# Norm rates on two columns: sums, reciprocal and root with tokens as rows, spread by a product with the identity

## The reference

```python
def _rmsnorm(x, w):
    xf = x.astype(jnp.float32)
    y = xf * lax.rsqrt(jnp.mean(xf * xf, axis=-1, keepdims=True) + RMS_EPS)
    return (y * w.astype(jnp.float32)).astype(x.dtype)

# first_block
    y = jnp.concatenate([_rmsnorm(y_ssm, ssm_out_norm_w[l]), _rmsnorm(y_mla, mla_out_norm_w[l])], axis=-1)
    h = h + y @ w_out[l]
    h = h + _conv_ffn(_rmsnorm(h, ffn_norm_w[l]), ffn_w_up[l], ...)
    return _rmsnorm(h, final_norm_w)
# second_block
    u = rms_norm(h, norm1_g[l])
    P = u @ w_in[l]
    ...
    v = rms_norm(h, norm2_g[l])
    h = h + (jax.nn.silu(v @ w_gate[l]) * (v @ w_up[l])) @ w_down[l]
    return rms_norm(h, norm_f_g)
```

## Time and profile before

| | |
|---|---|
| timed runs | 2952.76, 2955.98, 2956.33 us, median 2955.98 |
| span of the profiled execution | 2954.4 us |
| TensorE busy | 2857.8 us, 97% |
| VectorE busy | 2039.6 us, 69% |
| ScalarE busy | 1552.7 us, 53% |
| GpSimd busy | 724.2 us, 25% |
| chain that ended last | TensorE 78%, VectorE 10%, ScalarE 4%, GpSimd 4% |

### The profile page before, as it was taken

How to read it: one execution, slowest core, us unless ns; L and a number is a source line. 1 busy time by engine, 2 the same in 40 slices (tenths; PEclk the granted TensorE clock), 3 DMA queues, 4 the chain that set the end, 5 groups by cost and what they waited for, 6 DMA issues and landing times.

```text
span 2954.4 us, 52371 instructions
## 1 busy us (share of the span) xinstructions
PE 2857.8 (97%) x21074; PEld 2538.4 (86%) x21074; DVE 2039.6 (69%) x3273; ACT 1552.7 (53%) x2574; POOL 724.2 (25%) x870
## 2 busy tenths in 40 slices
PE   8989999999999998999899999999999999999998
PEld 8868988888888888888788888997888888888887
DVE  6675887765777667777777776777766665566654
ACT  7345555544555554566556655465445444444443
POOL 0342211200112230776456630003121110011112
PEclk9999999999999999999999999999999999999999
DMA  6314555556555555422222223454555555655554
GB/s 248 104 59 156 174 197 186 191 174 205 189 195 186 175 196 179 143 91 94 80 94 94 105 94 120 154 185 157 185 183 189 192 188 174 207 194 186 185 181 148
DMA packets 80046, 475.38 MB, mean 161 GB/s; under 512 B 8256, under 2 KB 11328, under 8 KB 38720
## 3 DMA queue, kind: packets, MB, share of 16 engines
q1 hardware_dynamic: 76768, 459.72, 45.0%
q10 hardware_dynamic: 3040, 12.32, 1.2%
HBM read 465.72 MB, written 6.29 MB: 160 GB/s over the span
## 4 chain that ended last, share of the span: by engine, by line
PE 78%; DVE 10%; ACT 4%; POOL 4%; issue 3%; DMA 0%; SPq 0%; POOLq 0%; ACTq 0%; DVEq 0%
PE bank L769 36%; PE bank L773 22%; PE bank L771 5%; PE bank L772 4%; PE bank L762 3%; DVE m L1307 2%; ACT m L2200 2%; POOL m L2933 2%; POOL m L2929 1%; DVE m L1353 1%; DVE m L1975 1%; PE bank L1103 1%; PE bank L1215 0%; PE bank L1107 0%; PE bank L866 0%
## 5 line engine op out<-in xcount | busy, mean ns | idle before, releaser
L773 PE MATMUL bank<-m,m 128*128 128x256 f32 x6624 | 1860.5, 281 | 0.0
L769 PE MATMUL bank<-m,m 128*128 128x512 f32 x4736 | 1650.0, 393 | 10.8 <-DVE m L2072 5.7
L1307 DVE TENSOR_TENSOR m<-m,m 128x1024 fp32r<-128x1024 f32 (+1 forms) x912 | 1033.1, 1141 | 569.9 <-ACT m L2200 563.5
L773 PEld LDWEIGHTS bank<-m,m 128*128 128x128 f32 x6624 | 1252.2, 189 | 0.2
L2200 ACT ACTIVATE m<-m 128x1024 fp32r<-128x1024 f32 (+1 forms) x912 | 877.7, 976 | 641.8 <-PE bank L773 615.4
L769 PEld LDWEIGHTS bank<-m,m 128*128 128x128 f32 x4736 | 890.7, 188 | 211.0 <-DVE m L2072 5.9
L771 PE MATMUL bank<-m,m 128*128 128x256 f32 x1888 | 561.2, 297 | 23.5 <-DVE m L1307 20.1
L772 PE MATMUL bank<-m,m 128*128 128x256 f32 x1888 | 534.6, 283 | 0.0
L771 PEld LDWEIGHTS bank<-m,m 128*128 128x128 f32 x1888 | 361.6, 192 | 43.4 <-issue 31.3
L772 PEld LDWEIGHTS bank<-m,m 128*128 128x128 f32 x1888 | 361.8, 192 | 1.3
L2909 POOL TENSOR_TENSOR m<-m,m 128x256 fp32r<-128x256 f32 x44 | 63.4, 1441 | 547.7 <-ACT m L2491 547.7
(11 more groups left out here) (375 smaller groups left out, 2830.5 us busy)
## 6 DMA issues: line engine op xcount, KB each, us to landing
m<-in_w_up SPq DMA_DIRECT2D x88, 1024.0 KB, 4.8
m<-in_w_down SPq DMA_DIRECT2D x128, 704.0 KB, 4.0
m<-in_w_gu SPq DMA_DIRECT2D x88, 1024.0 KB, 4.8
m<-in_w_out SPq DMA_DIRECT2D x48, 1024.0 KB, 5.1
m<-in_w_krv SPq DMA_DIRECT2D x48, 1024.0 KB, 4.8
m<-in_w_xbc SPq DMA_DIRECT2D x24, 1024.0 KB, 4.8
m<-in_w_z SPq DMA_DIRECT2D x16, 1024.0 KB, 4.8
m<-in_w_in SPq DMA_DIRECT2D x14, 1024.0 KB, 6.1
```

Source lines behind the costliest of these rows:

```text
L769: pe.matmul(bank.rearrange("p (a b) -> p a b", a=2), hi, x, start=kc == L.k0, stop=False)
L773: m = pe.matmul(ps, lo, x[:, 0, :], start=False, stop=last)
L1307: v.tensor_tensor(lo_of(k), raw_of(k)[0], hi_of(k).bitcast(F32), SUB).then_inc(*lo_v(("lo", k)))
```

## The change

Six norms in five places (MLA output, SSM output, first feed-forward, the pair of final norm and second layer's first norm, second feed-forward) get their rate as the last norm has it: `sum_rows` in place of the product with ones, 128x2 instructions on VectorE and a 128x2 root on ScalarE, a new product on TensorE (`spread_rate`) that waits for the root, and a copy from PSUM on ScalarE (`spread_out`) that waits for the spread and then signals the rate. The first norm (`N_attn`) stays as it was. The spread stands in TensorE's order behind the first tile of the MLA output projection, behind the second tile of the SSM's, half a tile after the sum in the up projections, and two turns after the sums in the second mixer. In the pair all six VectorE instructions come in the first turn, ScalarE's roots come one turn earlier, and the final norm's output chunks begin one turn later. GpSimd's nine memsets move from the start of the second mixer to the start of the second down projection.

```diff
+            def sum_rows(N, total):
+                for hf in range(2):
+                    m = pe.matmul(banks[N.bank][:, hf:hf + 1], total[:, hf * 128:hf * 128 + 128], ones[:, 0:1],
+                                  start=True, stop=True)
+                return m
...
-                    pe.matmul(banks[N.bank][:, 0:T], ones, SUMMED[N.id], start=True, stop=True).then_inc(
-                        *norm_pe(("sq", N.q0 + 15)))
+                    sum_rows(N, SUMMED[N.id]).then_inc(*norm_pe(("sq", N.q0 + 15)))
+                yield
+
+            def spread_rate(N, root):
+                pe.wait_ge(*root_a[N.id,])
+                for hf in range(2):
+                    m = pe.matmul(banks[N.bank][:, hf * 128:hf * 128 + 128], root[:, hf:hf + 1].broadcast_to([128, 128]),
+                                  ident, start=True, stop=True)
+                m.then_inc(*rate_pe((N.id,)))
...
             def mla_out():
                 add_total(N_mla)
                 yield
-                yield from linear(L_out, nrhs, lambda kc: cut_of(N_mla, kc - 8),
-                                  free=[[mla_a["o", 12]], [mla_a["o", 13]]])
+                yield from mix((linear(L_out, nrhs, lambda kc: cut_of(N_mla, kc - 8),
+                                       free=[[mla_a["o", 12]], [mla_a["o", 13]]]), 1),
+                               (timed((0, spread_rates((N_mla, rt)))), 1))
...
             def out2(t):
                 if t == 0:
                     add_total(N_ssm)
+                elif t == 1:
+                    spread_rate(N_ssm, rt)
...
-                        (iter(()) if q else timed((1, add_sums(N_ffn))), 1)))
+                        (iter(()) if q else timed((1, add_sums(N_ffn)), (2, spread_rates((N_ffn, rt)))), 1)))
...
-            second_mixer(main(), block, tail, after, iter(range(8)), timed((1, add_sums(N_end, N_two))),
+            second_mixer(main(), block, tail, after, iter(range(8)),
+                         timed((1, add_sums(N_end, N_two)), (3, spread_rates((N_two, rt), (N_end, re_)))),
                          timed((CLOSING, chain(turn_dt(), turn_cb(), turn_x(0, 13)))))
...
-                        (iter(()) if q else timed((1, add_sums(N_ffn2))), 1)))
+                        (iter(()) if q else timed((1, add_sums(N_ffn2)), (2, spread_rates((N_ffn2, rt)))), 1)))
...
+                    v.tensor_scalar(rt, banks[N.bank][:, 0:2], 1.0 / N.n, N.eps, MUL, ADD).then_inc(
+                        *norm_v(("ms", N.id)))
+                    v.wait_ge(*norm_v.last)
+                    v.reciprocal(rt, rt).then_inc(*norm_v(("rc", N.id)))
                 yield
...
+                a.activation(rt, rt, ACT.Sqrt).then_inc(*root_a((N.id,)))
+                yield
+                spread_out(rl, N)
+
+            def spread_out(dst, N):
+                a.wait_ge(*rate_pe[N.id,])
+                a.activation(dst, banks[N.bank][:, 0:T], ACT.Copy).then_inc(*norm_a(("rr", N.id)))
...
             def both_rates():
                 yield
-                yield
                 a.wait_ge(*norm_v["rc", N_two.id])
-                a.activation(rl, rl, ACT.Sqrt).then_inc(*norm_a(("rr", N_two.id)))
-                a.activation(rr, rr, ACT.Sqrt).then_inc(*norm_a(("rr", N_end.id)))
+                a.activation(rt, rt, ACT.Sqrt).then_inc(*root_a((N_two.id,)))
+                a.activation(re_, re_, ACT.Sqrt).then_inc(*root_a((N_end.id,)))
+                yield
+                spread_out(rl, N_two)
+                spread_out(rr, N_end)
...
+            def clear():
+                g.wait_ge(*ffn_v["cv", 87])
+                g.wait_ge(*ffn_a["hi", 43])
+                g.wait_ge(*ffn_g["lo", 43])
+                for q in (XA, *gt, *bkx, *sbd):
+                    g.memset(q, 0.0).then_inc(*wkv_g(*([("zero",)] if q is sbd[-1] else [])))
...
                 run(linear(L_up[q], conv))
+                if q:
+                    clear()
                 run(linear(L_down[q], add_squares(N_end, N_two) if q else None))
```

More of the change, by code:

```diff
@@ L465, in program @@
         ms, rr, rl = alloc(T), alloc(T), alloc(T)
+        rows = alloc(4, 2)
+        rt, re_, rm_ = rows[:, 0, :], rows[:, 1, :], rows[:, 2, :]
         w12, omm = alloc(16), alloc(52)
@@ L790, in add_squares @@
                     add_square(N, i)
+            def sum_rows(N, total):
[3 more added lines that the diff above has]
+                return m
             def add_total(N):
                 pe.wait_ge(*(mla_g if N is N_mla else glu_g)["sum", 7])
-                pe.matmul(banks[N.bank][:, 0:T], ones, total_of(N)[0], start=True, stop=True).then_inc(
-                    *sum_pe((N.id,)))
+                sum_rows(N, total_of(N)[0]).then_inc(*sum_pe((N.id,)))
             def add_sums(*Ns):
@@ L1361, in rate @@
                 v.wait_ge(*(sum_pe[N.id,] if N in (N_mla, N_ssm) else norm_pe["sq", N.q0 + N.nk - 1]))
-                v.tensor_scalar(ms, banks[N.bank][:, 0:T], 1.0 / N.n, N.eps, MUL, ADD).then_inc(*norm_v(("ms", N.id)))
-                v.wait_ge(*norm_v.last)
-                v.reciprocal(rl, ms).then_inc(*norm_v(("rc", N.id)))
+                if N is N_attn:
+                    v.tensor_scalar(ms, banks[N.bank][:, 0:T], 1.0 / N.n, N.eps, MUL, ADD).then_inc(
+                        *norm_v(("ms", N.id)))
+                    v.wait_ge(*norm_v.last)
+                    v.reciprocal(rl, ms).then_inc(*norm_v(("rc", N.id)))
+                else:
+                    v.tensor_scalar(rt, banks[N.bank][:, 0:2], 1.0 / N.n, N.eps, MUL, ADD).then_inc(
+                        *norm_v(("ms", N.id)))
+                    v.wait_ge(*norm_v.last)
+                    v.reciprocal(rt, rt).then_inc(*norm_v(("rc", N.id)))
                 yield
@@ L1370, in both_rates @@
                 v.wait_ge(*norm_pe["sq", N_two.q0 + 15])
-                v.tensor_scalar(ms, banks[N_end.bank][:, 0:T], 1.0 / D, N_end.eps, MUL, ADD).then_inc(*norm_v())
+                v.tensor_scalar(re_, banks[N_end.bank][:, 0:2], 1.0 / D, N_end.eps, MUL, ADD).then_inc(*norm_v())
                 v.wait_ge(*norm_v.last)
-                v.reciprocal(rr, ms).then_inc(*norm_v())
-                yield
+                v.reciprocal(re_, re_).then_inc(*norm_v())
                 v.wait_ge(*norm_v.last)
-                v.scalar_tensor_tensor(out=rl, in0=banks[N_two.bank][:, 0:T], scalar=1.0 / D, in1=rr, op0=MUL,
+                v.scalar_tensor_tensor(out=rt, in0=banks[N_two.bank][:, 0:2], scalar=1.0 / D, in1=re_, op0=MUL,
                                        op1=MUL).then_inc(*norm_v())
                 v.wait_ge(*norm_v.last)
-                v.tensor_scalar(rl, rl, N_two.eps, None, ADD).then_inc(*norm_v())
+                v.tensor_scalar(rt, rt, N_two.eps, None, ADD).then_inc(*norm_v())
                 v.wait_ge(*norm_v.last)
-                v.reciprocal(ms, rl).then_inc(*norm_v(("rm",)))
-                yield
-                v.wait_ge(*norm_v["rm"])
-                v.tensor_tensor(rl, ms, rr, MUL).then_inc(*norm_v(("rc", N_two.id)))
-                yield
-                yield
-                yield
+                v.reciprocal(rm_, rt).then_inc(*norm_v())
+                v.wait_ge(*norm_v.last)
+                v.tensor_tensor(rt, rm_, re_, MUL).then_inc(*norm_v(("rc", N_two.id)))
+                for _ in range(6):
+                    yield
                 v.wait_ge(*norm_a["rr", N_end.id])
@@ L2939, in main @@
                 for b in range(8):
-                    if b == 0:
-                        g.wait_ge(*norm_v["lo", N_two.x0 + 15])
-                        for q in (XA, *gt, *bkx, *sbd):
-                            g.memset(q, 0.0).then_inc(*wkv_g(*([("zero",)] if q is sbd[-1] else [])))
                     if b >= 4:
```

11 lines of the change are left out of this document (8 added, 3 removed).

## The result

The changed kernel takes 2969.61 us (median of 4, 2968.61 to 2972.20), the kernel before 2956.15 us in the same comparison (2952.76 to 2957.81): a ratio of 1.0049, 95% interval 1.0035 to 1.0064. The forecast was 2953.3 us in a range from 2948.0 to 2958.5. The kernel became slower by half a per cent, and the time lies 11 us above the range.

What follows compares the result with a forecast made beforehand. TensorE, busy 97% of the span, was taken as the bound. The pair -5.1, MLA +0.6, SSM +0.75 and two feed-forwards +0.55 each sum to -2.65 us, taking 2955.98 to 2953.3 us; range 2948.0 to 2958.5.

Steps and rivals of the forecast that it cites:

- The change part by part: The prediction's pricing of each norm's sums, rate, root and spread, and of the moved zeros, before going place by place.
- The pair: Final norm and second layer's first: 7.0 us early at 1127, 1.8 given back near 1137, net -5.1 us.
- the 2.7 us that the forecast took for the clock: In the pair: 26 half-clock matmuls behind the second hole, each 0.104 us slower, would return to full clock.
- MLA: MLA output norm: a new 1.3 us TensorE wait for the root, a later chain 0.6 us longer: +0.6 us.
- rival (a): Full recovery: nothing given back in the pair (-1.8), full clock behind the MLA waits (-2.1): 2949.4 us, chance 0.22.
- SSM: SSM output norm: spread 0.55 plus 0.2 us of waiting for VectorE's later weight cut: +0.75 us.
- First and second feed-forward: Norms in the up projections: no wait for the root, only the spread's work, +0.55 us each.
- The spread: New work in TensorE's own stream, taken as 0.55 us with the entry (bounds 0.45 and 1.04), six times: 3.3 us.
- Zeros: Nine GpSimd memsets moved to the second down projection, beside weight cuts: the move was to cost nothing there.
- (b): Rival, slower: the pair's gain is handed back whole at 1143.80, +2.45 us remains: 2958.4 us, chance 0.14.
- (c): Rival, nothing moves: the second layer's later waits absorb the gain as it meets the spreads: 2956.0 us, chance 0.16.

Runs made afterwards that it cites:

- b1: The kernel before with every tile, activations and weights alike, 32 bytes lower: 2954.4 us in one execution.
- c4: The kernel before with only the tile streamed by the feed-forwards' down projections, and the buffers behind it, 32 bytes further up: 2963.14 us.
- b2: The kernel before with 96 unused bytes per partition at the new tile's place, first run: 2969.91 us.
- d3: The kernel before with 96 unused bytes per partition at the new tile's place, the same kernel run again: 2976.08 us.

## Why the prediction was wrong

**The step that failed is the list of what the change adds.** "The change part by part" prices sums, rate, root, spread and zeros and closes with a sum; the new tile isn't in it, so its price was nothing. With it fell the premise of the first paragraph, that "only what fills or opens a hole on TensorE, or adds work to it, moves the end". 4480 blocks (4736 less the state space output's 256, which had the longer pitch already) became 6.6 ns longer each, 29.6 us, without a hole and without work; the narrow linears gave part of that back. The change has the line, though its excerpt under "The change" leaves it out, and in the kernel the names of the tiles that TensorE streams stand behind it. No row of the trace of before prices such a move, except one that I didn't look for: the state space output ran at 353.3 ns beside 346.7 for the same form of block elsewhere. A range that holds a cost of unknown size would have had to start from that.

The rest, place by place in the changed kernel and, where the move hides it, in the run without the move:

- **The pair**, -5.1 (its terms, 7.0 and 1.8, give -5.2): -5.24 in both, against the execution that the rows came from. By its parts: 6.66 us early at 1129.72 of the kernel before (forecast 7.0), 1.64 given back at 1143.80 (forecast 1.8); 6.49 and 1.25 without the move. No half clock follows the second hole, as the 6 us from its end show (columns as in the earlier trace rows):

```profile
1129.70:1135.70 6.00, 5.95 (x52) 5.98 (x53) 5.42 (x9) 2.41 (x3) 0.00 (x0) 1.00 0.51 175
```

  But the good match is in part luck. From its third to its twelfth piece the second mixer takes 34.23 us in the execution that the prediction read. In the nine other executions with these instructions it takes 30.85 to 33.32 us: 32.21 in b1 and 31.63 in c4, where the narrow linears keep their distance. With the new instructions it is 28.98 in the changed kernel and 28.99 without the move. In c4 the first hole is 1.36 us, not 2.62, and behind the second, as long as in the earlier trace rows, the clock is full (TensorE's busy time, clock, DMA):

```profile
1118.54 0.36 PE L771 MATMUL bank<-m,m 128*128 128x256 f32 x1 [1.36 <-DVE m L1307]
1124.67 0.36 PE L771 MATMUL bank<-m,m 128*128 128x256 f32 x1 [3.08 <-DVE m L1307]
1124.60:1130.60 6.00, 5.93 (x50) 1.00 0.53 175
```

  So the 2.7 us that the forecast took for the clock aren't lost in every execution, and the pair is worth 2.6 (against c4) to 5.2 us.

- **MLA**, +0.6: wrong in sign, -1.0 without the move. The chain came as described (table load to 275.81, root, spread, copy): it moved its end by 0.54 us, and TensorE's wait at its later place shrank from 2.15 to 0.72 us. What the sum put at nothing is the clock, which stood only in the bounds and in rival (a): the tile behind that wait took 1.6 us less. Before, TensorE idles, then runs 2.9 us at half clock; after, the half clock comes ahead of the root, where TensorE would have waited anyway, so the wait of 1.3 us for the root doesn't appear. TensorE's busy time and clock in the two places, before and after:

```profile
272.30:275.20 2.90, 2.63 (x21) 1.00 0.99 404
280.90:283.80 2.90, 2.90 (x15) 0.50 0.88 353
```
```profile
272.30:275.20 2.90, 2.90 (x13) 0.50 0.98 379
280.90:283.80 2.90, 2.90 (x28) 1.00 0.78 274
```

  That is one half of rival (a), which had 2.1 us for it; the other half, nothing given back in the pair, didn't come. The rule of the Trainium skill that the prediction weighed there (TensorE: Matmul & The Clock Gate, "What's actually happening") gave the right outcome at 280.9, a granted clock of 1.00; why the clock was low at 272.3 no row shows.
- **SSM**, +0.75: right, +0.72 by the fifth piece without the move; by the end of that linear it is +1.05 there and +0.71 with the memsets back. **First and second feed-forward**, +0.55 each: +0.37 and +0.46. The spread is mis-sized by 0.1 us: the block behind it starts 0.36 us later than without it and takes 0.44 in place of 0.35, so 0.45 in all, my lower bound. In the run with no tile moved:

```profile
377.80 0.61 PE L813 MATMUL bank<-m,m 128*128 128x128 f32 x4
378.16 0.48 PE L771 MATMUL bank<-m,m 128*128 128x512 f32 x1
...
378.60 0.39 PE L771 MATMUL bank<-m,m 128*128 128x512 f32 x1
```

  The forecast came from a row's busy time, which holds latency; the distance between starts of neighbours was the thing to take.
- **Zeros**: right. At their new place nine memsets (994.94, 4.28 us) run beside three cuts in 3.01 us.
- **Not forecast**: the last norm's spreads took 1.16 us in place of 2.08, and the kernel ends some 0.95 us sooner for it, and the second mixer behind the pair took 1.2 us back without the move. Neither is the change's: the two executions of one kernel, b2 and d3, have 1.16 and 2.07 us for these spreads, and b1 and c4, without the change, are 1.3 and 1.5 us longer than the kernel before in the second mixer behind the pair.

So the forecast of -2.65 and the -3.2 us without the move are near each other partly by luck: MLA came out 1.6 us lower, and the pair's 5.1 is the upper end of what it is worth.

The rivals: (b) and (c) were about the pair and fell, as without the move its gain of 5.24 us stands at 1143.80 and is not absorbed behind it beyond what executions differ by; the one that happened wasn't among them.

## What to carry to other kernels

When a change allocates a tile, list the tiles that move with it, and ask of each operand of the engine that sets the end where it lies afterwards; put small new tiles at the end of the memory, where no other tile moves, and the change is then priced by its instructions; padding to 128 bytes kept the pitch of the wide blocks here, but changed others. In a kernel whose bounding engine is never idle, compare the pitch of its repeated blocks before looking for holes: here 2% (346.7 against 353.3 ns) sat in every wide block. If two stages run the same form of block at two pitches, that is a hint that the layout has a price: moving operands made the changed kernel 12.7 us faster than the one before (2941.91 against 2954.64), where its instructions alone gave 3.2. And before a hole or a slow clock of a single trace goes into a sum, look whether it is there in a second execution.

## What the runs showed of the hardware

- TensorE's joined block (128x512 and 128x256 products with a weight load each) takes 346.7 or 353.3 ns at full clock, 16 cycles apart, also while no other engine and no DMA works. The place of the streamed operand against the weights decides: of the distances modulo 128, 32 gave the shorter pitch, 64 (four runs) and 96 (one run) the longer, in all up, gate and down projections that lay there; at 0 both were seen, from one execution to the next. With only the low or only the high half of the weights moved from 32 to 0, the pitch lay between, at 348.8 to 351.6 and 347.1 ns in the up and gate projections.
- A block of three 128x256 products prefers another distance: in the gates 342 to 343 ns at 64, 356 to 357 at 32 and 96, 361 at 0.
- More than the distance modulo 128 has a part: 128 more bytes between a narrow operand's halves undid its gain (355 ns at 64), and a move of all tiles by 128 bytes changed the state space output from 353.3 to 350.1 ns and the gates from 357 to 352.
- The clock behind a wait is not the same in every execution: behind the pair's second hole of 3.05 to 3.08 us the 6 us that follow had a granted clock of 0.50 in the kernel before, 0.72 in b1 and 1.00 in c4, with the same instructions; the hole some 6 us ahead of it was 2.62, 1.73 and 1.36 us.
